# Layer norm of the first two tiles spread over ScalarE, VectorE and GpSimd, in a two-layer streaming encoder

## The reference

```python
def layer_norm(x, g, b):
    xf = x.astype(jnp.float32)
    mu = jnp.mean(xf, axis=-1, keepdims=True)
    var = jnp.mean(jnp.square(xf - mu), axis=-1, keepdims=True)
    return ((xf - mu) * lax.rsqrt(var + LN_EPS) * g + b).astype(x.dtype)

for layer in range(DEPTH):                      # DEPTH = 2
    if layer % 2 == 0: out, ... = hybrid_mixer(x, ...)   # linear and latent attention
    else:              out, ... = pool_mixer(x, ...)     # trailing means, 4 windows
    x = layer_norm(ALPHA * x + out, ln_g[layer, 0], ln_b[layer, 0])
    ffn = moe_layer(x, ...)                              # 64 experts, top 8, + shared expert
    x = layer_norm(ALPHA * x + ffn, ln_g[layer, 1], ln_b[layer, 1])
```

## Time and profile before

| | |
|---|---|
| median of three runs | 1520.95 us (1519.12 to 1523.51) |
| the profiled execution, own time | 1521.64 us |
| its span, first to last instruction | 1519.9 us |
| PE busy | 1445.7 us (95%) |
| DVE busy | 637.1 us (42%) |
| ACT busy | 372.6 us (25%) |
| POOL busy | 45.4 us (3%) |
| mean granted TensorE clock | 0.938 of full |
| DMA | 435.34 MB, mean 286 GB/s over the span |

### The profile page before, as it was taken

How to read it: one execution, slowest core, us unless ns; L and a number is a source line. 1 busy time by engine, 2 the same in 40 slices (tenths; PEclk the granted TensorE clock), 3 DMA queues, 4 the chain that set the end, 5 groups by cost and what they waited for, 6 DMA issues and landing times.

```text
span 1519.9 us, 17857 instructions
## 1 busy us (share of the span) xinstructions
PE 1445.7 (95%) x6535; PEld 759.0 (50%) x6535; DVE 637.1 (42%) x1262; ACT 372.6 (25%) x746; POOL 45.4 (3%) x76
## 2 busy tenths in 40 slices
PE   6999899899999999999999877999999999999995
PEld 4565465464544544544454465544544544544542
DVE  0554532562433343343443557434433333433436
ACT  1341321421212212222221234112212212221213
POOL 4200100100000000000000010000000000000000
PEclk9996557999999999999999976999999999999998
DMA  9202020267998999999899822499989989998970
GB/s 286 69 6 111 8 90 0 89 270 283 392 392 347 411 392 380 374 395 389 352 412 390 348 74 83 174 372 376 392 365 392 390 352 411 389 394 364 396 315 31
DMA packets 63622, 435.34 MB, mean 286 GB/s; under 512 B 4323, under 2 KB 6435, under 8 KB 13536
## 3 DMA queue, kind: packets, MB, share of 16 engines
q1 hardware_dynamic: 60800, 427.21, 70.2%
q0 software_dynamic: 2784, 7.62, 1.7%
HBM read 433.06 MB, written 1.76 MB: 286 GB/s over the span
## 4 chain that ended last, share of the span: by engine, by line
PE 93%; DVE 5%; issue 1%; ACT 1%; DMA 1%; SPq 0%; DVEq 0%
PE bank L846 29%; PE bank L762 25%; PE bank L794 15%; PE bank L788 12%; PE bank L746 4%; PE bank L856 1%; PE bank L916 1%; DVE sb_ln_st L1484 1%; PE bank L1022 1%; PE bank L903 1%; DVE sb_x L1491 1%; DVE sb_x L1494 1%; PE bank L1145 1%; PE bank L1019 1%; PE bank L1015 1%
## 5 line engine op out<-in xcount | busy, mean ns | idle before, releaser
L1421 DVE TENSOR_TENSOR sb_x<-sb_x,bank 128x512 f32<-128x512 f32 (+1 forms) x396 | 242.1, 680 | 118.7 <-PE bank L788 118.7
L794 PE MATMUL bank<-sb_wslot,sb_ht 128*64 128x512 f32 x1024 | 231.0, 593 | 0.0
L846 PE MATMUL bank<-sb_wslot,sb_xg_own 128*64 128x512 f32 x1024 | 226.5, 595 | 1.7 <-ACT sb_xg_own L1197 1.7
L846 PE MATMUL bank<-sb_wslot,sb_xt 128*64 128x512 f32 x1024 | 226.8, 595 | 0.0
L1440 DVE TENSOR_TENSOR sb_hh<-sb_sg,bank 128x256 f32<-128x256 f32 x64 | 27.0, 422 | 375.7 <-ACT sb_sg L1221 375.7
L1427 DVE SCALAR_TENSOR_TENSOR sb_yl<-bank,sb_gslot,sb_yh 128x512 fp32r<-128x512 f32 x128 | 96.1, 751 | 162.7 <-ACT sb_yh L1203 162.7
L762 PE MATMUL bank<-sb_pick,sb_xh 128*128 128x512 f32 x432 | 160.8, 401 | 0.0
L788 PE MATMUL bank<-sb_yh,sb_place 128*128 128x512 f32 x396 | 157.5, 398 | 3.3 <-DVE sb_yl L1427 3.3
L1221 ACT ACTIVATE sb_sg<-bank 128x256 f32<-128x256 f32 x64 | 24.5, 384 | 550.0 <-PE bank L846 550.0
L788 PE MATMUL bank<-sb_yl,sb_place 128*128 128x512 f32 x396 | 156.7, 396 | 0.0
L794 PEld LDWEIGHTS bank<-sb_wslot,sb_ht 128*64 128x64 f32 x1024 | 72.8, 137 | 144.6 <-issue 139.3
(11 more groups left out here) (296 smaller groups left out, 1242.3 us busy)
## 6 DMA issues: line engine op xcount, KB each, us to landing
sb_wslot<-in_moe_w_gate_dram SPq DMA_DIRECT2D x64, 2048.0 KB, 8.0
sb_wslot<-in_moe_w_up_dram SPq DMA_DIRECT2D x64, 2048.0 KB, 12.7
sb_wslot<-in_moe_w_down_dram SPq DMA_DIRECT2D x64, 2048.0 KB, 15.0
sb_w_in_hi<-in_w_in_dram SPq DMA_DIRECT2D x2, 2048.0 KB, 22.3
sb_w_in_lo<-in_w_out_dram SPq DMA_DIRECT2D x1, 4096.0 KB, 13.4
sb_w_in_lo<-in_w_in_dram SPq DMA_DIRECT2D x2, 1024.0 KB, 11.1
sb_ln_g<-in_ln_g_dram POOLq DMA_DIRECT2D x4, 512.0 KB, 4.6
sb_ln_b<-in_ln_b_dram POOLq DMA_DIRECT2D x4, 512.0 KB, 6.1
```

The costliest lines, as they stand in the source:

```text
L794: last = pe.matmul(y_b[c][64 * e:64 * e + 64, :], ht[:, k, 64 * e:64 * e + 64], w_down[u][:, e, k * D + c * 512:k * D + (c + 1) * 512], st ...
L846: last = pe.matmul(gu_b[64 * e:64 * e + 64, :], xgt[b][:, k, sl], w_gu[u][:, :, e, k * FE:(k + 1) * FE], start=k == 0, stop=k == DK_SLICES ...
L1421: dve.tensor_tensor(dst, dst, banks.tile[order[f]][0:rows, :], ALU.add).then_inc(s["added"], 1)
```

## The change

ACT computes `ln_sd` = sqrt(var + eps) in place of the logarithm and the exponential, and DVE takes the reciprocal (`ln_rs`), for all three tiles. For tiles 0 and 1, DVE also computes `ln_nb` = -mean * rs, ACT normalises the tile in place (`Identity` with scale `ln_rs` and bias `ln_nb`), DVE multiplies it by `ln_g`, and POOL adds `ln_b`, which signals `x_ready`. Tile 2 keeps its two DVE passes; the second waits until POOL has signalled tile 1 (`x_ready` counts in order). Four table loads are requested by hand with one-column activations (`warm`). ACT's root of tile 2 of norms 0 and 2 moves behind its copies of the transposed tile 1. POOL takes each `shift(n)` ahead of the work that it has behind the norm. The arithmetic of the rest is unchanged.

```diff
+            def shift(n):
+                for t in range(2):
+                    gp.wait_ge(x_gained, 2 * n + t + 1)
+                    gp.tensor_tensor(x[:, t, :], x[:, t, :], ln_b[:, :], ALU.add).then_inc(x_ready, 1)
...
                     gp.memset(xt[:, :, T_COLS:], 0.0).then_inc(s["init"], 1)
 
+                    gp.wait_ge(ln_in, 32 * 2)
+                    shift(1)
                     gp.wait_ge(x_ready, 6)
...
                 else:
+                    gp.wait_ge(ln_in, 32)
+                    shift(0)
                     gp.wait_ge(x_ready, 3)
...
+                if l:
+                    gp.wait_ge(ln_in, 32 * 3)
+                    shift(2)
                 gp.wait_ge(x_ready, 3 + 6 * l)
                 load_ln(l, 1)
+            gp.wait_ge(ln_in, 32 * 4)
+            shift(3)
...
-            def ln_rsqrt(n, tiles=range(TILES)):
-                for t in tiles:
-                    rows = ROWS[t]
-                    act.wait_ge(var_ready, 3 * n + t + 1)
-                    rsqrt(ln_rs[0:rows, t:t + 1], ln_mv[0:rows, t, 1:2], 1.0, eps[0:rows, 0:1], rs_ready)
+            def warm(func):
+                step(act.activation(warmed[:, :], eps[:, 0:1], func))
+
+            def ln_sqrt(n, t):
+                rows = ROWS[t]
+                act.wait_ge(var_ready, 3 * n + t + 1)
+                act.activation(ln_sd[0:rows, t:t + 1], ln_mv[0:rows, t, 1:2], ACT.Sqrt, bias=eps[0:rows, 0:1]).then_inc(sd_ready, 1)
+                if t < 2:
+                    act.wait_ge(rs_ready, 2 * n + t + 1)
+                    act.activation(x[:, t, :], x[:, t, :], ACT.Identity, scale=ln_rs[:, t:t + 1], bias=ln_nb[:, t:t + 1]).then_inc(x_normed, 1)
...
-                ln_rsqrt(2 * l, (0, 1))
-                copy_xt(l + 1, (0, 1))
+                warm(ACT.Sqrt)
                 if l == 0:
                     act.wait_ge(stored, 16 * MIX_STORES)
+                ln_sqrt(2 * l, 0)
+                ln_sqrt(2 * l, 1)
+                copy_xt(l + 1, (0, 1))
                 split_high(0)
-                ln_rsqrt(2 * l, (2,))
                 copy_xt(l + 1, (2, 3))
+                ln_sqrt(2 * l, 2)
+                warm(ACT.Exp)
                 split_high(1)
...
-                ln_rsqrt(2 * l + 1)
+                warm(ACT.Sqrt)
+                for t in range(TILES):
+                    ln_sqrt(2 * l + 1, t)
...
-                for t in range(TILES + 1):
-                    if t < TILES:
-                        rows = ROWS[t]
-                        before(t, rows)
-                        for c in range(2):
-                            step(dve.bn_stats(ln_st[0:rows, t, c, :], x[0:rows, t, c * 512:(c + 1) * 512]))
-                        step(dve.bn_aggr(ln_mv[0:rows, t, :], ln_st[0:rows, t, :, :].rearrange("p a b -> p (a b)")), var_ready)
+                def scale(t):
+                    rows = ROWS[t]
+                    dve.wait_ge(sd_ready, 3 * n + t + 1)
+                    step(dve.reciprocal(ln_rs[0:rows, t:t + 1], ln_sd[0:rows, t:t + 1]))
+                    if t < 2:
+                        dve.tensor_scalar(ln_nb[0:rows, t:t + 1], ln_mv[0:rows, t, 0:1], ln_rs[0:rows, t:t + 1], -1.0,
+                                          ALU.mult, ALU.mult).then_inc(rs_ready, 1)
+
+                def gain(t):
+                    dve.wait_ge(x_normed, 2 * n + t + 1)
+                    dve.tensor_tensor(x[:, t, :], x[:, t, :], ln_g[:, :], ALU.mult).then_inc(x_gained, 1)
+
+                for t in range(TILES):
+                    rows = ROWS[t]
+                    before(t, rows)
+                    xr = x[0:rows, t, :]
+                    for c in range(2):
+                        step(dve.bn_stats(ln_st[0:rows, t, c, :], x[0:rows, t, c * 512:(c + 1) * 512]))
+                    step(dve.bn_aggr(ln_mv[0:rows, t, :], ln_st[0:rows, t, :, :].rearrange("p a b -> p (a b)")), var_ready)
                     if t == 0:
                         dve.wait_ge(ln_in, 32 * (n + 1))
-                    else:
-                        rows = ROWS[t - 1]
-                        xr = x[0:rows, t - 1, :]
-                        step(dve.scalar_tensor_tensor(out=xr, in0=xr, scalar=ln_mv[0:rows, t - 1, 0:1], in1=ln_g[0:rows, :],
-                                                      op0=ALU.subtract, op1=ALU.mult))
-                        dve.wait_ge(rs_ready, 3 * n + t)
-                        step(dve.scalar_tensor_tensor(out=xr, in0=xr, scalar=ln_rs[0:rows, t - 1:t], in1=ln_b[0:rows, :],
-                                                      op0=ALU.mult, op1=ALU.add), x_ready)
+                        scale(0)
+                    if t == 1:
+                        gain(0)
+                        scale(1)
+                gain(1)
+                step(dve.scalar_tensor_tensor(out=xr, in0=xr, scalar=ln_mv[0:rows, 2, 0:1], in1=ln_g[0:rows, :],
+                                              op0=ALU.subtract, op1=ALU.mult))
+                scale(2)
+                dve.wait_ge(x_ready, 3 * n + 2)
+                step(dve.scalar_tensor_tensor(out=xr, in0=xr, scalar=ln_rs[0:rows, 2:3], in1=ln_b[0:rows, :],
+                                              op0=ALU.mult, op1=ALU.add), x_ready)
```

More of the change, by code:

```diff
@@ L319, in build @@
         ln_rs = sb("ln_rs", [P, TILES])
+        ln_sd = sb("ln_sd", [P, TILES])
+        ln_nb = sb("ln_nb", [P, TILES])
+        warmed = sb("warmed", [P, 1])
         eps = sb("eps", [P, 2])
@@ L524, in build @@
         var_ready = sem("var_ready")
+        sd_ready = sem("sd_ready")
         rs_ready = sem("rs_ready")
+        x_normed = sem("x_normed")
+        x_gained = sem("x_gained")
         x_ready = sem("x_ready")
```

## The result

The changed kernel takes 1527.67 us (median of 6 runs, 1524.21 to 1530.90). The kernel before took 1520.65 us beside it (6 runs, 1518.73 to 1523.52). The ratio is 1.0044, with a 95% interval from 1.0025 to 1.0063. The profiled executions agree: 1529.32 us with a span of 1527.5, against 1521.64 and 1519.9.

The account below looks back on a forecast made before the run. PE bounds the kernel (93% of the span), and only four DVE stretches at the norms can move: 2.4 + 2.3 + 2.5 + 1.0 = +8.2 on 1520.95, about 1529.2 us, range 1521.5 to 1534.5.

Parts of the forecast that it names:

- PE waits for tile 1 in norms 0 to 2, and DVE's last pass in norm 3: At the four norms, the only places the change can move: +2.4, +2.3, +2.5 and +1.0 us.
- The price of an add: GpSimd's add of `ln_b`, 1024 columns: 2.24 us, plus 0.29 to the waiter, 2.53 in all, between 0.98 and 2.95.
- Held for the full length: At each norm, the add of tile 1 stands behind the whole 1.28 us of tile 2's first DVE pass.
- the one row of 5.16: Profile row: DVE's one-input pass over 640 columns took 5.16 us beside POOL's clear, ending 0.35 behind it.
- `gain(1)` held by the add of tile 0, L1748 held by 0.5 in norm 2: DVE's `gain(1)` waits for tile 0's add; norm 2's last tile 2 sum, with two SBUF inputs, waits 0.5 us.
- What is hidden: Behind the norms: tile 2 about 4.5 us behind tile 1, later loads, clears and hand-made table loads cost nothing.
- Rival 1: At the norms, DVE and POOL read side by side, nothing held: +2.6 us, 1523.5; chance 0.28.
- Rival 2: In norms 1 to 3 the add of tile 0 also holds the `ln_nb` product: +1.8 each, 1534.5 us; chance 0.12.
- Rival 3: Behind norms 1 and 2, shifted starts return the full clock early: -3.3 us at norm 2, 1514 in all; chance 0.06.

Follow-up runs that it names:

- experiment 1: Changed kernel, but DVE's first pass over tile 2 waits until POOL has added tile 1: 1527.03 us, ratio 1.0053 to the kernel before.
- experiment 2: Changed kernel with tile 2's first pass waiting for POOL's add and two dummy one-input statistics operations over tile 2 in its place: 1527.62 us, one run.
- experiment 3: Changed kernel with tile 2's passes rearranged, so that DVE only subtracts the mean (one wide input) beside the add: 1523.72 us, one run.
- experiment 5: Kernel before with only the root changed: square root on ACT, reciprocal on DVE, both passes still on DVE in the old order: 1520.76 us, ratio 1.0010.
- experiment 4: Changed kernel with the add of `ln_b` given back to DVE, POOL doing nothing at the norms: 1524.15 us, ratio 1.0030 to the kernel before.
- experiment 6: Kernel before with the square root and reciprocal, each tile normalised at once, ACT's work reordered to suit: 1516.10 us, ratio 0.9966.
- experiment 7: Kernel before with each tile normalised at once and ACT's work reordered, but the old logarithm and exponential kept: 1526.48 us, ratio 1.0046.
- experiment 8: Kernel before with 8 dummy matmuls of 512 columns in PE's idle time ahead of norm 1's first mix: 1520.58 us, ratio 0.9993.

## Why the prediction was right

The forecast was slower by 8.2 in the direct terms, 1529.2 us; 1527.67 came. The steps, one by one:

- **PE waits for tile 1 in norms 0 to 2, and DVE's last pass in norm 3.** So it is, with GpSimd as the releaser. Forecast +2.4, +2.3, +2.5 and +1.0; measured +1.9, +2.1, +2.3 and +0.8. The sum is 7.2 in place of 8.2.
- **The price of an add.** 2.24 was taken and 2.35 measured. The 0.29 from its end to the waiter was wrong: 0.06, from 289.31 + 3.31 = 292.62 to 292.68. That row measured POOL's own DMA behind its clear, not another engine's wait. This and the next step make the way of tile 1, from the end of `gain(1)` to the waiter, 0.3 to 0.4 shorter than forecast in each norm (3.44 to 3.50 in place of 3.85). In norms 1 to 3 some 0.2 of it is lost again ahead of `gain(1)`'s end (in norm 1 7.34 behind aggregate 0 in place of 7.16). Together that is the 1.0 that the sum is too high.
- **Held for the full length.** The add of tile 1 did start behind tile 2's pass, and was held. A pass of 1.27 cost it 0.96 in place of 1.28: 0.16 of the pass lay ahead of the add's start, and the add needs 2.20 once the pass has ended, not 2.35. Experiments 1 to 3 show the cause by taking the pass away, and by replacing it with one that doesn't hold and one that does. The choice of the full length, made from the one row of 5.16, was right, though that row is a one-input pass, of the kind of experiment 3.
- **`gain(1)` held by the add of tile 0, L1748 held by 0.5 in norm 2.** 1.67 and 1.92 in place of 1.22 and 1.22, so L1748 by 0.7.
- **What is hidden.** Tile 2 of norm 0 was ready at 297.03, and PE took it at 299.04. The experts of layer 0 took 570.14 against 570.18, so the later loads cost nothing. That the square root takes nothing off the path is experiment 5.
- **Rival 1, nothing is held:** false, 3.31 against 2.35. **Rival 2, the product for `ln_nb` is held:** it didn't come, 0.21. But in norms 1 to 3 the product started 0.04 ahead of the add (878.95 and 878.99 in norm 1), and not while it ran, as the rival has it. What becomes of one that comes later no run shows. A one-column reciprocal that did start beside the add (883.64 in norm 1) took its usual 0.15.
- **Rival 3, the clock.** The stretches behind the norms do move with the clock, but not as forecast. It put -3.3 behind norm 2 and as much behind norm 1, or +3.3 behind norm 0. Behind norm 1 it was +1.9, behind norm 2 -1.0, behind norm 0 +0.3. The +1.9 is no consequence of GpSimd's add alone: experiments 4 and 5 have it too.
- **What was luck.** The sum puts the stretches between the norms at nothing. In the trace they hold entries of up to 1.9, which come to +0.5, the clock's among them. That they nearly cancel was not forecast, and in experiments 6 and 7 they don't (+8.4 and +4.5 in the traces).

What stays open: experiment 1 made tile 1 ready 1 us earlier in three norms, and the total is no shorter. Its ten runs lie between 1519.05 us at a mean clock of 0.940 and 1532.01 at 0.932, and what decides between such clocks no trace shows. So the 7.2 are shown in the trace, norm by norm; that each of them counts in full in the runs is not. The ratios stand in the expected order (1.0044 with GpSimd's adds, 1.0030 with DVE's in their place, 1.0010 with the root alone), but the intervals of neighbours overlap.

## What to carry to other kernels

Splitting a pass over engines pays only if the way from the last statistics to the waiting engine gets shorter; a smaller share of DVE alone gains nothing: here 2.56 on one engine became 1.23 there and 3.31 on another. Before giving a wide operation that reads two tensors to GpSimd, list what DVE runs beside it, and count each pass with two SBUF inputs, or in the fast one-input form, at nearly its full length (here 1.27 cost the add 0.96, and 0.74 cost it 0.43). And when a small operation becomes cheap (a root without table loads), look at the order that was built to hide its old price: here only both together gained.

## What was not expected of the hardware

- GpSimd's add of 128x1024 float32 takes 2.35 alone. Where a DVE pass held it, it ends 2.20 after that pass. A DVE pass that was held by the add ends 1.08 after it (881.34 to 882.42).
- The first add of the changed kernel started 0.50 after `gain(0)` had ended (281.60 to 282.10); the others 0.07 to 0.15 after it. It cost nothing, since PE was busy.
- The clock fell from 2.4 to 1.2 GHz with PE at work throughout, in the 64-column matmuls: at 893 in experiment 8, and at 891 in the kernel before, where the same pairs go from 0.38 to 0.63. Keeping PE busy ahead of norm 1 kept the full clock through the first mixing matmuls and until 893, no longer.
- The length of the wait ahead of norm 1 doesn't order the time of the mixing behind it: 9.48 and 16.94 in experiment 3, 7.75 and 20.09 in experiment 5.
